# Sliding-window attention on one core: a step that handles two heads, with matmuls that alternate between halves of the PE array

## What is computed

```python
def window_attention(q, k, v, k_ctx, v_ctx, sink):          # for each block of 128 queries
    s_lat = where(valid, q_block @ k_near.T * scale, -inf)  # keys at most 128 tokens away
    s_ctx = q_block @ k_ctx.T * scale                       # 256 context keys
    p = softmax(concatenate([sink_col, s_lat, s_ctx]))      # the sink takes weight, has no value
    return p_lat @ v_near + p_ctx @ v_ctx
def context_attention(q, k, v, sink):                       # the two blocks of context queries
    p = softmax(concatenate([sink_col, q @ k.T * scale]))[..., 1:]
    return p @ v
```

## Time and profile before

| what | value |
|---|---|
| median of 3 runs | 4421.15 us (4418.71 to 4421.94) |
| the profiled execution's own time | 4422.47 us |
| its span in the trace | 4420.7 us, 50903 instructions |
| busy share of the span | PE 93%, PEld 73%, DVE 51%, ACT 32%, POOL 7% |
| mean granted PE clock | 0.938 of full speed |
| first matmul of `window_stage` to its last output copy | 367.0 to 506.2 us |

### The profile page before, as it was taken

How to read it: one execution, slowest core, us unless ns; L and a number is a source line. 1 busy time by engine, 2 the same in 40 slices (tenths; PEclk the granted TensorE clock), 3 DMA queues, 4 the chain that set the end, 5 groups by cost and what they waited for, 6 DMA issues and landing times. The chain is left out here.

```text
span 4420.7 us, 50903 instructions
## 1 busy us (share of the span) xinstructions
PE 4103.7 (93%) x21109; PEld 3229.5 (73%) x21109; DVE 2252.7 (51%) x3396; ACT 1426.6 (32%) x2086; POOL 316.0 (7%) x314
## 2 busy tenths in 40 slices
PE   7998899999999999899999799889998979888998
PEld 4875667888878777578778388558786658656876
DVE  5625765554553332542463565743574455464366
ACT  2114532111442222432351222432462132242264
POOL 0000120000000000000000332000000223100000
PEclk9997879999999999999999899789999989889998
DMA  5500012343111111122222000023222100012321
GB/s 201 165 20 9 6 39 96 118 140 105 60 60 65 65 65 55 58 86 95 87 94 72 6 1 1 6 73 98 86 89 83 34 6 1 6 39 72 93 93 67
DMA packets 254722, 288.92 MB, mean 65 GB/s; under 512 B 6756, under 2 KB 226939, under 8 KB 254517
## 3 DMA queue, kind: packets, MB, share of 16 engines
q1 hardware_dynamic: 252437, 281.84, 19.6%
q10 hardware_dynamic: 2080, 4.19, 0.3%
HBM read 283.92 MB, written 2.10 MB: 65 GB/s over the span
## 5 line engine op out<-in xcount | busy, mean ns | idle before, releaser
L458 PE MATMUL banks<-h_halves,w_halves 128*128 128x512 f32 x3824 | 1432.6, 375 | 83.1 <-DVE h_halves L257 42.2
L459 PE MATMUL banks<-h_halves,w_halves 128*128 128x512 f32 x3824 | 1426.2, 373 | 0.0
L460 PE MATMUL banks<-h_halves,w_halves 128*128 128x512 f32 x3824 | 1419.1, 371 | 0.0
L458 PEld LDWEIGHTS banks<-h_halves,w_halves 128*128 128x128 f32 x3824 | 733.0, 192 | 223.3 <-issue 73.6
L460 PEld LDWEIGHTS banks<-h_halves,w_halves 128*128 128x128 f32 x3824 | 730.2, 191 | 126.9
L459 PEld LDWEIGHTS banks<-h_halves,w_halves 128*128 128x128 f32 x3824 | 733.0, 192 | 120.8
L257 DVE TENSOR_TENSOR w_halves<-work,w_halves 128x2048 fp32r<-128x2048 f32 (+1 forms) x215 | 488.2, 2271 | 472.0 <-ACT w_halves L252 472.0
L252 ACT ACTIVATE w_halves<-work 128x2048 fp32r<-128x2048 f32 (+1 forms) x215 | 407.2, 1894 | 586.6 <-PE banks L460 452.7
L252 ACT ACTIVATE h_halves<-kept 128x512 fp32r<-128x512 f32 (+1 forms) x520 | 332.5, 666 | 315.6 <-PE banks L460 236.3
L257 DVE TENSOR_TENSOR h_halves<-kept,h_halves 128x512 fp32r<-128x512 f32 (+1 forms) x520 | 361.3, 736 | 139.3 <-ACT h_halves L252 138.6
L947 DVE SCALAR_TENSOR_TENSOR kept<-kept 128x512 f32<-128x512 f32 x280 | 188.2, 744 | 7.0 <-DMA kept<-in_mod_w 7.0
(11 more groups left out here) (357 smaller groups left out, 4968.5 us busy)
## 6 DMA issues: line engine op xcount, KB each, us to landing
work<-in_w_ff SPq DMA_DIRECT2D x64, 1024.0 KB, 5.3
work<-in_ffn_w_in SPq DMA_DIRECT2D x44, 1024.0 KB, 5.0
kept<-in_mod_w SPq DMA_DIRECT2D x40, 1024.0 KB, 5.1
work<-in_odd_w_in SPq DMA_DIRECT2D x24, 1024.0 KB, 5.2
work<-in_w_in SPq DMA_DIRECT2D x24, 1024.0 KB, 4.9
work<-in_ffn_w_out SPq DMA_DIRECT2D x16, 1024.0 KB, 5.4
work<-in_even_w_in SPq DMA_DIRECT2D x13, 1024.0 KB, 5.1
work<-in_odd_w_out SPq DMA_DIRECT2D x8, 1024.0 KB, 5.3
```

Source lines behind the costliest of these rows:

```text
L458: nc.tensor.matmul(o, low[:, k - a, fc], rh[:, tc], start=(k == 0), stop=False)
L459: nc.tensor.matmul(o, high[:, k - a, fc], rl[:, tc], start=False, stop=False)
L460: mm = nc.tensor.matmul(o, high[:, k - a, fc], rh[:, tc], start=False, stop=(k == K - 1))
```

## The change

The same stage, rewritten around a step that takes one tile, and so both of its heads: 24 steps (`steps = [(p, i) ...]`) instead of 48, again in cycles of six.

- `scores` issues the matmuls of the even head (array rows 0 to 63) and of the odd head (rows 64 to 127) in turn: both masks, even context, odd window, even window, a wait for the even context scores, odd context. The wait is there because both context results share a bank. A step's scores lie in three banks, and all that follows sees them as one region for each head.
- `weigh` goes through the key blocks and for each issues the even head's matmuls (array columns 0 to 63) and then the odd one's (columns 64 to 127). Each head has its own order of key blocks (`values`), as its scores lie.
- The transposes of the 10, 8 or 4 blocks of a step go in three, three or two chunks (`chunk_widths`), alternating between banks 6 and 7; each chunk has a copy of its own on ACT. The weighing of step s-1 stands between the first and the second chunk of step s. The output of a weighing sits in the last quarter of the bank of a later chunk (`out_chunk`, `hosted`), with waits that keep the two apart.
- On DVE the maximum is one reduction with two results for each partition, the small operations work on two columns at once, the multiplication is one instruction for each head with a semaphore each (the first chunks wait only for the even head), and `out` copies 128 partitions at once, one step later than before. There is one small addition more in each step (score maximum plus sink), which lets ACT do the sinks of both heads in one instruction.
- `pr` and `pt` are twice as wide.

```diff
-    steps = [(h, i) for h in range(8) for i in range(6)]
+    steps = [(p, i) for p in range(4) for i in range(6)]
...
+    chunk_widths = {5: (4, 3, 3), 4: (3, 3, 2), 2: (2, 2)}
...
+    out_chunk = lambda s: first_chunk[s + 1] + 1 if s < N - 1 else len(chunks)
+    hosted = {out_chunk(s): s for s in range(N)}
+    turn_bank = lambda g: 6 + g % 2
+    out_at = lambda s: core.ps[:, turn_bank(out_chunk(s)), 3 * P:4 * P]
...
             def scores(s):
...
-                    pe.wait_ge(exped, s - 1)
-                n = len(ks)
-                if n:
-                    lat = core.ps[:, (s % 2) * 2, 512 - n * P:512]
-                    nc.tensor.matmul(lat, ident16, mask16[:, m0:m0 + n * P], start=True, stop=False)
-                    nc.tensor.matmul(lat, q, k[hh, CTX + ks[0] * P:CTX + (ks[0] + n) * P], start=False, stop=True)
-                nc.tensor.matmul(core.ps[:, (s % 2) * 2 + 1, 0:CTX], q, k[hh, 0:CTX], start=True,
-                                 stop=True).then_inc(scored, 1)
+                    pe.wait_ge(exped, 2 * (s - 1))
+                if n == 0:
+                    nc.tensor.matmul(bank(1, 0, CTX), q[0], k[0][:, 0:CTX], start=True, stop=True)
+                    nc.tensor.matmul(bank(2, 0, CTX), q[1], k[1][:, 0:CTX], start=True, stop=True).then_inc(scored, 1)
+                    return
+                lat = [bank(0, 512 - n * P, n * P), bank(2, 0, n * P)]
+                near = slice(CTX + ks[0] * P, CTX + (ks[0] + n) * P)
+                for f in range(2):
+                    nc.tensor.matmul(lat[f], ident16, mask16[:, m0:m0 + n * P], start=True, stop=False)
+                nc.tensor.matmul(bank(1, 0, CTX), q[0], k[0][:, 0:CTX], start=True, stop=True).then_inc(ctx_scored, 1)
+                nc.tensor.matmul(lat[1], q[1], k[1][:, near], start=False, stop=True)
+                nc.tensor.matmul(lat[0], q[0], k[0][:, near], start=False, stop=True)
+                pe.wait_ge(ctx_scored, p * 4 + i - 1)
+                nc.tensor.matmul(bank(1, CTX, CTX), q[1], k[1][:, 0:CTX], start=True, stop=True).then_inc(scored, 1)
+
+            def turn(g):
+                s, b, w = chunks[g]
+                pe.wait_ge(normalised_even, s + 1)
+                if b + w > blocks(s):
+                    pe.wait_ge(normalised_odd, s + 1)
+                if g >= 2:
+                    pe.wait_ge(turned_copied, g - 1)
+                if g - 2 in hosted:
+                    pe.wait_ge(out_done, hosted[g - 2] + 1)
...
             def weigh(s):
...
-                for j, t in enumerate(vt):
-                    mm = nc.tensor.matmul(o, vtok[:, t * P + kv * HD:t * P + (kv + 1) * HD],
-                                          pt[s % 2][:, j * P:(j + 1) * P], start=(j == 0), stop=(j == len(vt) - 1))
+                pe.wait_ge(turned_copied, first_chunk[s] + len(chunk_widths[n]))
...
+                for j in range(n):
+                    for f in range(2):
+                        t = values(s)[f][j]
+                        mm = nc.tensor.matmul(out_at(s)[f * HD:(f + 1) * HD], vtok[:, t * P + kv * HD:t * P + (kv + 1) * HD],
+                                              pt[s % 2][:, (f * n + j) * P:(f * n + j + 1) * P], start=(j == 0),
+                                              stop=(j == n - 1))
...
             for s in range(N):
                 if s + 2 < N:
                     scores(s + 2)
+                g = first_chunk[s]
+                turn(g)
                 if s:
                     weigh(s - 1)
-                turn(s)
+                turn(g + 1)
+                if len(chunk_widths[blocks(s)]) == 3:
+                    turn(g + 2)
```

More of the change, by code:

```diff
@@ L1565, in keys, with blocks, values @@
         return ks, (ks[0] - b + 1) * P
+    def blocks(s):
+        return len(keys(steps[s][1])[0]) + 2
     def span(s):
-        n = len(keys(steps[s][1])[0])
-        o = (s % 2) * 1024
-        return flat[:, o + 512 - n * P:o + 768], n
+        o, n = (s % 2) * 1536, blocks(s) - 2
+        if n == 0:
+            return flat[:, o + 512:o + 1536].rearrange("p (h k) -> p h k", h=2)[:, :, 0:CTX]
+        return flat[:, o + 512 - n * P:o + 1024 + n * P].rearrange("p (h k) -> p h k", h=2)
+    def values(s):
+        ks = [2 + k for k in keys(steps[s][1])[0]]
+        return [ks + [0, 1], [0, 1] + ks if ks else [0, 1]]
+    chunk_widths = {5: (4, 3, 3), 4: (3, 3, 2), 2: (2, 2)}
+    chunks, first_chunk = [], []
+    for s in range(N):
+        first_chunk.append(len(chunks))
+        b = 0
+        for w in chunk_widths[blocks(s)]:
+            chunks.append((s, b, w))
+            b += w
+    out_chunk = lambda s: first_chunk[s + 1] + 1 if s < N - 1 else len(chunks)
+    hosted = {out_chunk(s): s for s in range(N)}
+    turn_bank = lambda g: 6 + g % 2
+    out_at = lambda s: core.ps[:, turn_bank(out_chunk(s)), 3 * P:4 * P]
     with nc.Block() as block:
@@ L1575, in scores @@
             def scores(s):
-                h, i = steps[s]
+                p, i = steps[s]
                 ks, m0 = keys(i)
-                hh = slice((h % 2) * HD, (h % 2 + 1) * HD)
-                q = tiles[h // 2][hh, i * P:(i + 1) * P]
-                k = kdup[h // 4]
+                n = len(ks)
+                q = [tiles[p][f * HD:(f + 1) * HD, i * P:(i + 1) * P] for f in range(2)]
+                k = [kdup[p // 2][f * HD:(f + 1) * HD] for f in range(2)]
+                bank = lambda b, a, w: core.ps[:, (s % 2) * 3 + b, a:a + w]
@@ L1599, in turn @@
                 mm.then_inc(turned, 1)
             def weigh(s):
[L1602 to L1609, removed]
[L1610 to L1612 removed]
+                p, _ = steps[s]
@@ L1653, in _ @@
                     exps(s + 1)
-                copy(s)
+                for g in range(first_chunk[s], first_chunk[s] + len(chunk_widths[blocks(s)])):
+                    copy(g)
         @block.vector
@@ L1672, in normalise @@
+                chain.wait()
+                nc.vector.tensor_tensor(small(s, 2), core.sb(SINK0 + 2 * p, 2), small(s, 1), ALU.add).then_inc(maxed, 1)
             def normalise(s):
-                _, n = span(s)
-                dve.wait_ge(exped, s + 1)
-                chain(nc.vector.tensor_tensor(small(s, 4), small(s, 2), small(s, 3), ALU.add))
+                L = blocks(s) * P
+                dve.wait_ge(exped, 2 * (s + 1))
+                chain(nc.vector.tensor_tensor(small(s, 5), small(s, 4), small(s, 3), ALU.add))
@@ L1676, in normalise @@
                 chain.wait()
-                chain(nc.vector.reciprocal(small(s, 5), small(s, 4)))
+                chain(nc.vector.reciprocal(small(s, 6), small(s, 5)))
                 chain.wait()
-                p = pr[s % 2][:, 0:(n + 2) * P]
-                nc.vector.tensor_scalar(p, p, small(s, 5), None, ALU.mult).then_inc(normalised, 1)
+                for f, done in enumerate((normalised_even, normalised_odd)):
+                    half = pr[s % 2][:, f * L:(f + 1) * L]
+                    nc.vector.tensor_scalar(half, half, small(s, 6)[:, f:f + 1], None, ALU.mult).then_inc(done, 1)
@@ L1691, in _ @@
                     top(s + 1)
+                if s >= 2:
+                    out(s - 2)
                 normalise(s)
-                if s:
-                    out(s - 1)
+            out(N - 2)
             out(N - 1)
```

59 lines of the change are left out of this document (33 added, 26 removed).

## The result

The changed kernel takes 4373.5 us as the median of 4 runs (4369.56 to 4379.83), and the kernel before, beside it, 4420.42 (4418.71 to 4421.94). The ratio is 0.9895, with a 95% interval of 0.9878 to 0.9912. It is faster by 46.9 us where 30.5 were forecast, and lies 8.5 us under the lower end of the range. The direction was right, the size was not.

What follows compares the result with a forecast made beforehand. PE's issue rate was taken to bound the stage. Four cycles 8.2 us shorter give 32.8, less 1.5 for the ends and 0.8 for waits in the scores: 30.5, so 4391 us, range 4382 to 4406.

Steps and rivals of the forecast that it cites:

- my 0.47: Clock in the stage: each us at 1.2 GHz loses about 0.47 us after the change, 0.46 before.
- the ends: Stage's first step and last copies, with nothing to hide them: a one-time cost of 1.5 us, bounds 0.5 and 3.
- the wait in the middle of the scores: Wait inside a scores group for a result ending half a group earlier: 0 to 0.1 us in 16 steps, 0.8 taken.
- The rule for two halves: Scores and weighing on PE: a matmul starts once its half is free and the one ahead in the program has started.
- 0.18: Weighing: the odd head ends some 0.18 us behind the even one, so two heads take 1.42, 1.20 and 0.76.
- With a slow stretch of the same 20 us nothing changes: Stage's start at 1.2 GHz: if the slow stretch stays 20 us, the clock adds 0 to the forecast.
- Half as long would give 5 us: Stage's start: a slow stretch half as long gives 5 us; this case is in the range's lower end, 4382.
- The rival of a clock that stays low: Stage never leaves 1.2 GHz and takes 181 us instead of 139, so 4463 us; chance 0.04.
- nothing outside it moves but by time shifts: Rest of the kernel: the change touches one stage only, 139 us of 4421; all else only shifts in time.
- Softmax and copies: Rival in the stage: softmax and copies become the bound, a cycle takes some 26.5 us, so 4402 us; chance 0.12.
- one alternation alone: Rival: only rows or only columns overlap, a cycle takes 26.1 or 27.4 us, so 4401 or 4405; chance 0.05.
- none: Rival: neither alternation overlaps, a cycle takes 29.9 us and 6 us are gained, so 4415 us; chance 0.04.

Runs made afterwards that it cites:

- e1_rows: Changed kernel with the even head's window scores issued ahead of the odd head's, so the heads' score matmuls no longer alternate; 4374.80 us (one run).
- e2_cols: Changed kernel with the weighing taking all key blocks of the even head first, then all of the odd head; 4387.62 us (one run).
- e11_pairs: Changed kernel with the weighing alternating between the heads every two key blocks instead of every one; 4371.11 us (one run).
- e12_threes: Changed kernel with the weighing alternating between the heads every three key blocks instead of every one; 4376.47 us (one run).
- e4_weigh_first: Changed kernel with the weighing of the previous step put ahead of the first chunk of transposes; 4367.16 us (one run).
- e5_dve: Changed kernel with DVE's output copy moved from ahead of the normalisation to between its two multiplications; 4367.70 us, ratio 0.9889 to the kernel before.
- e3_both: Changed kernel where neither scores nor weighing alternate: even window scores ahead of odd, and all even-head key blocks weighed first; 4381.24 us (one run).
- e8_before_warm: Kernel before the change with six extra matmuls of a constant in the stage ahead, results unread; 4424.16 us.
- e6_warm: Changed kernel with six extra matmuls of a constant in the stage ahead, results unread; 4372.91 us, ratio 1.0007 to the changed kernel.
- e9_no_overlap: Changed kernel with PE waiting for the even head's matmuls to end before the odd head's, in scores and weighing; 4435.03 us (one run).
- e13_dve_first: Changed kernel with DVE's output copy between the two multiplications and the weighing ahead of the first chunk of transposes; 4377.37 us.

## Why the prediction was off

**The accounting.** The stage was to shrink by 30.5 us and shrank by 42.8. Four cycles of 31.80 less 22.19 give 38.4, where 32.8 stood. The slow stretch is 10.0 us shorter, by my 0.47 worth 4.7, where 0 stood. What is left, 0.3, are the ends, where 2.3 stood with the wait in the middle of the scores (which turned out to lie inside the cycle). The three differences, 5.6, 4.7 and 2.0, are the 12.3 us that the stage's term was short.

**The rule for two halves failed.** The first failing step is "a matmul starts when its half is free and the one ahead of it in the program has started". The trace of the changed kernel itself has a row of the odd half (421.38) that starts before the even half's row ahead of it (421.69). e1_rows shows a matmul that starts before the one ahead of it, and e2_cols, e11_pairs and e12_threes that PE looks past some three unstarted rows of the other half. From that rule came two terms. One is the "0.18" by which the odd head was to end behind the even one. The weighings took 1.24, 1.03 and 0.59 instead of 1.42, 1.20 and 0.76, 5.72 a cycle and not 6.76. The other is the scores: 1.38 with 3 window blocks and with 2, and 0.65 with none (read in e4_weigh_first), instead of 1.62, 1.40 and 0.96. With masks (0.42 and 0.31, as forecast) a cycle's scores take 8.28 and not 9.40. That 1.40 came so close for 2 window blocks is luck: the odd half starts 0.3 us earlier than the rule has it, and loses 0.21 to the wait for the even context scores. The transposes came out at 6.22, forecast 6.26.

**The waits were larger.** PE's sum is thus 5.72 + 8.28 + 6.22 = 20.22, forecast 22.42. The cycle takes 22.19, so the waits are 2.0 and not 1.2, still inside their bounds of 0.9 and 3. The place was half right. Of the two steps with 5 key blocks only the second waits, for 0.9 us; the other wait, as long, is at the step with 4 blocks behind it, and the first of the two waits for under 0.1. The cause given, the maximum of the next step ahead of the normalisation, was incomplete. The output copy that waits for ACT ahead of it adds more, as e5_dve shows: moving it took 1.48 us off the cycle.

**The clock.** "With a slow stretch of the same 20 us nothing changes" failed in its condition, and the reserve beside it, "Half as long would give 5 us", is what happened. The price per slow us holds in two comparisons. Between e2_cols and e3_both, with equal cycles, 3.4 us less of it shorten the stage by 1.76, 0.5 each; between before and e8_before_warm 7.1 us more lengthen it by 3.3, 0.47 each. It fails in a third: e6_warm has 6.7 us less than the changed kernel and a stage only 1.9 shorter, 0.3 each. Most of the part that went lies in the start-up, where PE waits for the first softmax besides, which fits a lower price but isn't tested. In all eleven profiles of kernels whose halves overlap the stretch was 3.5 to 10.3 us, in the three without 20 to 38. The rival of a clock that stays low was thus wrong in sign: I reasoned that a shorter cycle has a larger part of waits. What in the overlap brings the clock back earlier is open. e9_no_overlap has the same start-up with pairs as the changed kernel and 37.5 us, so the pairs' start alone is not the cause.

**The ends.** They cost 0.3 and not 1.5. The stage less four cycles is 7.7 us after and 12.05 before. The slow stretches, at 0.47, are 4.8 and 9.5 of these, which leaves 2.9 and 2.6. The wait in the middle of the scores, priced at 0.8 us in all, costs 1.7: nothing with 3 window blocks, 0.21 us with 2. PE as a whole shows no gap ahead of L1620, since the even half works on; the wait is inside the 1.38 us of the set.

**Outside the stage.** The profiled executions differ by 49.3 us of own time, 6.5 more than the stage, and the medians by 46.9, 4.1 more. The prediction had "nothing outside it moves but by time shifts". The span less the stage is 4281.5 us for before, 4275.0 for the changed kernel in its first profile and 4281.0 in its second, and 4270.4 to 4281.7 over all profiles. One kernel thus differs from run to run by nearly as much as the 6.5. These differences go with the time at a granted clock of 0.50 outside the stage: 501 us of it in the first profile of the changed kernel and 521 in the second, 525 in that of before, and 471 in e5_dve, which has the 4270.4. The medians of the changed kernel were 46.9 and 47.2 below before on two chips, some 4 us more than the stage. But the interval of the ratio is a gain of 39 to 54 us, which holds the stage's 42.8, and e13_dve_first gained 1.7 us less than its stage. So a steady gain outside the stage is not shown.

**The rivals.** Softmax and copies didn't become the bound: DVE is busy for 75% of a cycle and ACT for 68%. The Trainium skill's rule in "TensorEngine Tiling (Array Packing)", section "PSUM Bottleneck", binds the change only by way of DVE. PE itself waits for no copy of ACT's, but DVE's output copy does and holds the normalisation behind it, for up to 1.48 us a cycle (e5_dve). It binds e4_weigh_first and e13_dve_first directly, by the 1.58 us of PE's waits for ACT in a cycle. Neither one alternation alone nor none came about. e9_no_overlap gives the second a price: 32.70 us a cycle, where I had worked out 29.9 and a gain of 6. Its one run is 15.3 us slower than the kernel before beside it, but 17.3 us more of slow clock, 8 us at 0.47, are in that. The added waits are some 1.5 of its cycle, so it is an upper bound for a chip whose halves don't overlap, and 31.2 is the estimate without them. The saved starts that I had counted on do not show in it.

**What was right.** PE's issue bound the stage; both alternations overlap; the f32 column halves, which the trace of before didn't have, run at the full 0.055 us per trace row inside a group; the instruction counts and prices of ACT, DVE, masks and transposes held to within 1 us a cycle.

## What to carry to other kernels

Two heads whose matmuls use different halves of the array, by rows or by columns, cost the time of one or little more, f32 included, if they alternate at least every two matmuls: 1.24 us for 1.24 in the weighing, 1.38 for 1.27 in the scores with 3 window blocks. A semaphore between the halves can take part of it back (1.38 for 1.06 with 2 window blocks). The order may be loose by a few rows, so let other needs (banks, masks) set it. Once PE's time is no longer the sum of its matmuls, look at which small instruction stands ahead of the one that PE waits for: moving a single output copy on DVE by one place was worth 1.5 us in 22, and a second edit that was good alone spoiled it, so try such edits together before adding up their gains.

## What was unexpected of the hardware

- Starts of matmuls are not in program order across halves: in e1_rows a matmul of the odd half started at 419.62 and the one ahead of it in the program, for the even half, at 420.14. The Trainium skill, in "TensorE: Matmul & The Clock Gate", section "The mechanism", says that matmuls start and end in program order, without reordering. The trace of this kernel disagrees for the starts.
- The look-ahead is short, three rows as these runs have it. With ten rows of one half queued ahead, the other half's first row started only 0.71 us into the group, with three rows unstarted.
- Both rows of an f32 matmul and the other half's share the array without loss: 20 rows of 64 columns, ten for each half, in 1.24 us; ten of one half alone in 1.24.
- The low clock that follows the stage's start lasted 3.5 to 10.3 us with overlap and 20 to 38 without, and matmuls without use ahead of the stage did not take it away (3.5 us with overlap, 27.3 without).
